# A hybrid block whose expert layer handles 56 instead of 48 tokens by gathered rows, with the choice of experts begun in the query projection

## The reference

```python
q = (xb @ w_q).reshape(T, PEER_HEADS, 2, PEER_HALF)            # 8 heads, 2 halves of 128
sc = jnp.einsum('thcd,hckd->thck', q, sub_keys)                # 128 keys for each half
s1, i1 = lax.top_k(sc[:, :, 0], PEER_TOPK)                     # the best 16 of each half
s2, i2 = lax.top_k(sc[:, :, 1], PEER_TOPK)
cand = (s1[..., :, None] + s2[..., None, :]).reshape(T, PEER_HEADS, PEER_TOPK * PEER_TOPK)
best, ci = lax.top_k(cand, PEER_TOPK)                          # the best 16 of 256 sums
...
u_sel = jnp.take(u_tab, idx, axis=0)                           # 128 rows of 16384 for each token
act = jax.nn.gelu(jnp.einsum('td,thkd->thk', xb, u_sel))
v_sel = jnp.take(v_tab, idx, axis=0)
return jnp.einsum('thk,thkd->td', g.astype(act.dtype) * act, v_sel)
```

## Time and profile before

| what | us |
|---|---|
| median of 3 runs | 1776.24 |
| lowest and highest | 1774.4, 1777.46 |
| the profiled execution: its own time | 1771.97 |
| its span, first to last instruction | 1769.7 |
| scoring's first product | 450.2 |
| value stage's first product | 1125.3 |

### The profile page before, as it was taken

How to read it: one execution, slowest core, us unless ns; L and a number is a source line. 1 busy time by engine, 2 the same in 40 slices (tenths; PEclk the granted TensorE clock), 3 DMA queues, 4 the chain that set the end, 5 groups by cost and what they waited for, 6 DMA issues and landing times. The chain is left out here.

```text
span 1769.7 us, 28855 instructions
## 1 busy us (share of the span) xinstructions
PE 1744.7 (99%) x10950; PEld 1655.2 (94%) x10950; DVE 1423.8 (80%) x2151; ACT 931.9 (53%) x1403; POOL 415.8 (23%) x293
## 2 busy tenths in 40 slices
PE   9999999999999999999999999999999999999997
PEld 7887778788999999999999999999999999999997
DVE  4556786575589899999999998688888888888995
ACT  5454574444456555555555545555555545555553
POOL 0002300020142133111111112023434433343341
PEclk9999999999999999999999999999999999999998
DMA  7765455678577677777777779899999999999992
GB/s 233 213 188 167 143 150 178 184 255 236 172 218 219 218 256 243 253 240 230 230 227 228 232 232 324 254 338 373 353 357 344 356 325 356 360 368 403 366 347 85
DMA packets 127138, 462.59 MB, mean 261 GB/s; under 512 B 14864, under 2 KB 14944, under 8 KB 126352
## 3 DMA queue, kind: packets, MB, share of 16 engines
q1 hardware_dynamic: 95760, 347.65, 60.5%
q0 software_dynamic: 30960, 112.64, 17.1%
q10 hardware_dynamic: 288, 0.55, 0.1%
HBM read 455.73 MB, written 5.05 MB: 260 GB/s over the span
## 5 line engine op out<-in xcount | busy, mean ns | idle before, releaser
L1641 PE MATMUL PS<-W,HI 128*128 128x416 f32 x2048 | 438.9, 354 | 1.4 <-DVE W L1222 0.8
L1601 PE MATMUL PS<-xT,HI 128*128 128x416 f32 x2048 | 438.4, 356 | 0.0
L682 ACT ACTIVATE HI<-V_RAW 128x1024 fp32r<-128x1024 f32 x256 | 271.7, 1062 | 282.6 <-PE PS L1641 151.4
L1641 PEld LDWEIGHTS PS<-W,HI 128*128 128x128 f32 x2048 | 366.1, 189 | 7.2 <-DVE OUTA L1256 1.9
L1601 PEld LDWEIGHTS PS<-xT,HI 128*128 128x128 f32 x2048 | 366.0, 189 | 2.9
L1146 DVE TENSOR_TENSOR V_LO<-V_RAW,HI 128x2048 fp32r<-128x2048 f32 x128 | 293.0, 2289 | 48.6 <-ACT HI L682 43.4
L682 ACT ACTIVATE HI<-RING_RAW 128x1024 fp32r<-128x1024 f32 x256 | 269.6, 1053 | 77.5 <-DMA RING_RAW<-u_t 72.0
L1153 DVE TENSOR_TENSOR RING_LO<-RING_RAW,HI 128x1024 fp32r<-128x1024 f32 x232 | 274.4, 1219 | 4.6 <-ACT HI L682 4.6
L819 DVE TENSOR_TENSOR LO<-RAW,HI 128x1024 fp32r<-128x1024 f32 x132 | 163.1, 1238 | 142.8 <-PE PS L1349 97.9
L1607 PEld LDWEIGHTS PS<-xT,RING_LO 128*128 128x128 f32 x2048 | 268.0, 191 | 3.7 <-DVE RING_LO L1153 2.2
L1646 PEld LDWEIGHTS PS<-W,V_LO 128*128 128x128 f32 x2048 | 269.4, 191 | 1.9 <-DVE V_LO L1146 0.8
(11 more groups left out here) (209 smaller groups left out, 1656.9 us busy)
## 6 DMA issues: line engine op xcount, KB each, us to landing
RING_RAW<-u_t SPq DMA_DIRECT2D x256, 512.0 KB
V_RAW<-peer_v SPq DMA_DIRECT2D x256, 512.0 KB
RAW<-w_in SPq DMA_DIRECT2D x80, 512.0 KB, 3.7
RAW<-w_out SPq DMA_DIRECT2D x32, 512.0 KB, 4.4
RAW<-wq_t SPq DMA_DIRECT2D x32, 512.0 KB, 4.8
x_spill<-X POOLq DMA_DIRECT2D x2, 1024.0 KB, 5.8
X1R<-x_spill POOLq DMA_DIRECT2D x8, 256.0 KB
X<-x SPq DMA_DIRECT2D x3, 512.0 KB, 8.4
```

The source lines that it names most:

```text
L682: nc.scalar.activation(HI[:, n % HI_SLOTS, :], raw_of(n), ACT.Copy).then_inc(top_ready, 1)
L1601: return mm(PS[:, j % S_BANKS, 0:2 * ND].rearrange("p (a t) -> p a t", a=2), HI[:, n % HI_SLOTS, kk * P:(kk + 1) * P], xT[:, k, :, 0:ND], ...
L1641: return mm(PS[:, V_BANKS[i], 0:2 * ND].rearrange("p (a t) -> p a t", a=2), HI[:, v % HI_SLOTS, i * P:(i + 1) * P], weights_of(v), start=v ...
```

## The change

NB_ goes from 16 to 24, so 56 tokens are gathered and ND is 200. The 24 tokens of B stand five times in 120 partitions, with 26 groups of picks instead of 16; half rows go from 192 to 232, of which 78 are in scoring. The order of the halves is now A's dots, A's sums, B's dots, B's sums (`half_of`), with two small activations (`A_GELU_AT` is step 111). The key scores are taken in the query projection, two columns of keys after every fourth unit (`pair_scores`), and the first 12 pieces of both tiles' choice run there on DVE; the other 58 pieces run in the steps 1 to 39. For the units 9, 11, ... 31 of the query projection POOL makes the low part instead of DVE. The loads of the keys move ahead for that. Spreading is the steps 43 to 92; `one_hots` is one comparison for both tables on DVE, and ACT multiplies the second by the gates in four operations (`gates_into`). It stands ahead of `apply_gates` now. The loops of the query projection are written out. Not shown: places in memory, semaphores, and the constants' other uses.

```diff
-NA, NB_ = 32, 16
+NA, NB_ = 32, 24
 NS = NA + NB_
 ND = T - NS
-GROUPS_A, GROUPS_B = P * NA // P, P * NB_ // P
+PICKS = PH * TOPK
+ROWS_A, ROWS_B = P // NA, P // NB_
+PB = ROWS_B * NB_
+GROUPS_A, GROUPS_B = PICKS // ROWS_A, -(-PICKS // ROWS_B)
 NG = GROUPS_A + GROUPS_B
-PICKS = PH * TOPK
...
-CHOICE0 = 2
-GATES_AT = (20, 48)
-PICKS_AT = (31, 58)
-ROWS_SAVED_AT, ROWS_BACK_AT = 32, 35
+EARLY = 12
+QUERY_BESIDE = range(WQ0 + 9, WQ_END, 2)
+CHOICE0 = 1
+
+
+def piece_steps():
+
+    steps, j = [], CHOICE0
+    rest = 2 * (PIECES - EARLY)
+    while len(steps) < rest:
+        steps += [j] * min(2 - j % 2, rest - len(steps))
+        j += 1
+    return [-1] * EARLY + steps[:PIECES - EARLY] + [-1] * EARLY + steps[PIECES - EARLY:]
+
+
+PIECE_STEPS = piece_steps()
+PIECE_COUNT = {j: PIECE_STEPS.count(j) for j in range(NKEYS)}
+PLAIN_STEP = {j: PIECE_COUNT[j] > 0 and all(k % PIECES in PLAIN for k in range(2 * PIECES) if PIECE_STEPS[k] == j)
+              for j in range(NKEYS)}
+BEST_PIECE = HC + 2 + PH
+GATES_AT = tuple(PIECE_STEPS[o * PIECES + BEST_PIECE] + 1 for o in range(TT))
+PICKS_AT = tuple(PIECE_STEPS[o * PIECES + PIECES - 1] + 2 for o in range(TT))
+ROWS_SAVED_AT, ROWS_BACK_AT = PICKS_AT[0] + 1, PICKS_AT[0] + 4
 TOKB = 4
 N_BATCH = ND // TOKB
-SPREAD0 = 60
+SPREAD0 = PICKS_AT[1] + 2
 SPREAD_END = SPREAD0 + N_BATCH
 FIRST_WEIGHTS_AT = SPREAD_END + 2
...
-HALF_STEPS = list(range(40, SPREAD0, 3)) + list(range(SPREAD0, SPREAD_END, 2)) + list(range(SPREAD_END, NKEYS - 7))
+HALF_STEPS = sorted([j for j in range(SPREAD0 - 3, SPREAD_END) if j % 3] + list(range(SPREAD_END, NKEYS - 7))
+                    + list(range(SPREAD_END, NKEYS - 7, 2)))
...
+A_DOTS, A_SUMS = 2 * GROUPS_A, 4 * GROUPS_A
+B_DOTS, B_SUMS = A_SUMS + 2 * GROUPS_B, A_SUMS + 4 * GROUPS_B
+A_GELU_AT = HALF_STEPS[A_DOTS - 1]
+B_GELU_AT = HALF_UNITS[B_DOTS - 1 - len(HALF_STEPS)]
+
+
+def half_of(k):
+
+    if k < A_SUMS:
+        return k < A_DOTS, k % A_DOTS // 2, k % 2
+    return k < B_DOTS, GROUPS_A + (k - A_SUMS) % (2 * GROUPS_B) // 2, k % 2
...
+            def keys(q):
+                pool.dma_start(KEYS[:, 4 * q:4 * q + 4, :], keys_t[:, 4 * q:4 * q + 4, :]).then_inc(keys_ready[q], 16)
+
+            pool.wait_ge(used, WQ0 + 1)
+            keys(0)
             pool.wait_ge(used, WQ0 + 2)
             for half in range(2):
                 cols = slice(half * HALF, (half + 1) * HALF)
                 pool.dma_start(FGAIN[:, cols], ffn_gain[:, cols].broadcast_to([P, HALF])).then_inc(fgain_ready, 16)
+            pool.wait_ge(used, WQ0 + 5)
+            keys(1)
...
-            for q in range(4):
-                pool.wait_ge(used, WQ0 + 14 + 2 * q)
-                pool.dma_start(KEYS[:, 4 * q:4 * q + 4, :], keys_t[:, 4 * q:4 * q + 4, :]).then_inc(keys_ready, 16)
-            pool.wait_ge(xg_saved, 16)
-            for r in range(P // NA):
-                pool.wait_ge(used, WQ0 + 22 + 2 * r)
-                pool.dma_start(X4[r * NA:(r + 1) * NA, :], xg_dram[0:NA, :]).then_inc(x4_ready, 16)
+            for n in QUERY_BESIDE:
+                pool.wait_ge(hi_ready, n + 1)
+                pool.wait_ge(used, n - (LO_SLOTS - 1))
+                nc.gpsimd.tensor_tensor(LO[:, n % 2, :], RAW[:, n % 4, :], HI[:, n % 4, :].bitcast(FP32),
+                                        ALU.subtract).then_inc(lo_ready[n % 2], 1)
+                if n == WQ0 + 9:
+                    keys(2)
+                if n == WQ0 + 17:
+                    keys(3)
+                if n - WQ0 in (21, 23, 25, 27):
+                    r = (n - WQ0 - 21) // 2
+                    pool.wait_ge(xg_saved, 16)
+                    pool.dma_start(X4[r * NA:(r + 1) * NA, :], xg_dram[0:NA, :]).then_inc(x4_ready, 16)
...
+            def pair_scores_out(q):
+
+                act.wait_ge(sc_done, q + 1)
+                nc.scalar.activation(SC[:, :, 2 * q:2 * q + 2, :],
+                                     PS[:, 4 + q % 4, :].rearrange("p (t a b) -> p t a b", t=TT, b=NKEYS), ACT.Copy)\
+                    .then_inc(sc_out, 1)
+
+            for m in range(4, N_WQ):
+                hi(WQ0 + m)
+                if m >= 9 and m % 4 == 1:
+                    pair_scores_out((m - 9) // 4)
...
+            def gates_into(b):
+
+                act.wait_ge(compared, b + 1)
+                for i in range(TOKB):
+                    t = b * TOKB + i
+                    ins = nc.scalar.activation(ONE[:, 1, i, :], ONE[:, 1, i, :], ACT.Copy, scale=EG[:, 2, t:t + 1])
+                ins.then_inc(ones, 1)
...
+            dve.wait_ge(xs_saved, 16)
+            for m in range(2, N_WQ + 2):
+                if m < N_WQ:
+                    lo(WQ0 + m)
+                c = (m - 3) // 2
+                if m % 2 and c >= 0:
+                    dve.wait_ge(used, WQ0 + 2 * c + 2)
+                    add_halves(QTQ[:, c, :], c % 2)
+                if m % 2 == 0 and 0 <= (m - 8) // 2 < EARLY:
+                    for o in range(TT):
+                        next(pieces[o])
+                        done[o] += 1
...
-                v.tensor_tensor(ONE1[:], IOTA[:].unsqueeze(1).broadcast_to([P, TOKB, NKEYS]),
-                                EG[:, 0, b * TOKB:(b + 1) * TOKB].unsqueeze(2).broadcast_to([P, TOKB, NKEYS]), ALU.is_equal)
-                for i in range(TOKB):
-                    t = b * TOKB + i
-                    ins = v.tensor_scalar(ONE2[:, 4 * i:4 * i + 4, :], IOTA[:].rearrange("p (q c) -> p q c", q=4),
-                                          EG[:, 1, t:t + 1], EG[:, 2, t:t + 1], ALU.is_equal, ALU.mult)
-                ins.then_inc(ones, 1)
+                t0 = b * TOKB
+                v.tensor_tensor(ONE[:], IOTA[:].unsqueeze(1).unsqueeze(1).broadcast_to([P, 2, TOKB, NKEYS]),
+                                EG[:, 0:2, t0:t0 + TOKB].unsqueeze(3).broadcast_to([P, 2, TOKB, NKEYS]), ALU.is_equal)\
+                    .then_inc(compared, 1)
...
-                if 0 <= b < N_BATCH:
-                    apply_gates(b)
                 if 0 <= b + 1 < N_BATCH:
                     assert done == [PIECES, PIECES]
                     one_hots(b + 1)
+                if 0 <= b < N_BATCH:
+                    apply_gates(b)
                 if b >= 0:
                     land(j)
-                if j in HALF_STEPS:
-                    half_rows(HALF_STEPS.index(j))
+                for k in range(len(HALF_STEPS)):
+                    if HALF_STEPS[k] == j:
+                        half_rows(k)
...
+            def pair_scores(q):
+
+                pe.wait_ge(tile_out, 2 * q + 2)
+                pe.wait_ge(keys_ready[q // 2], 16)
+                if q >= 4:
+                    pe.wait_ge(sc_out, q - 3)
+                for tt in range(TT):
+                    for c in (2 * q, 2 * q + 1):
+                        at0 = (2 * tt + c % 2) * NKEYS
+                        last = mm(PS[:, 4 + q % 4, at0:at0 + NKEYS], QTQ[:, c, tt * P:(tt + 1) * P], KEYS[:, c, :],
+                                  start=True, stop=True)
+                last.then_inc(sc_done, 1)
+
+            for m in range(N_WQ):
+                n = WQ0 + m
+                high_ready(n)
+                if m >= 4 and m % 2 == 0:
+                    pe.wait_ge(tile_out, m // 2 - 1)
+                column_unit(n, m // 2 % 2, low_ready(n),
+                            (lambda k: pe.wait_ge(tr_lo, 16 + max(2, k // 2 + 1))) if m < 2 else None)
+                if m >= 5 and m % 4 == 1:
+                    pair_scores((m - 5) // 4)
```

190 lines of the change are left out of this document (69 added, 121 removed).

## The result

The changed kernel takes **1810.88 us** (median; 1805.77 to 1811.19) and the kernel before 1775.32 beside it: ratio 1.0195, 95% interval 1.0171 to 1.022. Forecast were 1758.3 us and a range of 1747 to 1769. It is slower by 1.7 to 2.2%, and yet the profile says that its products did get cheaper.

What follows compares the result with a forecast made beforehand. The prediction took PE's own pace as the bound, busy for 1744.7 of 1769.7 us. Its terms summed to -17.9 us, which from the median of 1776.24 gave 1758.3 us, range 1747 to 1769.

Steps and rivals of the forecast that it cites:

- high products, both stages: Scoring and value stage: 4096 high products on PE move 16 columns fewer, 6.5 ns each, -26.6 us.
- low products: Scoring and value stage: low products go from 208 to 200 columns but stand on a floor, 0.
- choice on DVE: Scoring steps 24 to 28: DVE's sums of the choice run late and PE waits, +4 us.
- query: wait and clock: Query projection: PE stalls for POOL's first low part, +5.0 us, and the pause lowers its clock, +1.7.
- spreading's new loop: Spreading steps: the chain through DVE and ACT takes 5.5 us of a 5.6 us step and fits narrowly, 0.
- gathered halves, late: Scoring steps 93 to 119: three halves take 10.0 us against 9.44; between 0 and +4, taken as +2 us.
- value stage: Value stage: 154 halves instead of 150, loads and gathers at 364 GB/s where they were 352, costing 0.
- -1.8: Spreading: 50 batches instead of 52, 16 products fewer at 113 ns, -1.8 us.
- -2.2: Scoring: PE's old waits where the second tile's sums are chosen go away, -2.2 us.
- were it 0.15 longer: Spreading: with the loop 0.15 us longer, 50 steps would lose 7.5 us, less nearly 3 that PE's order leaves.
- more waits: Rival: the loop through ACT (+5), or gathers at the upper bound with a longer choice stall; 1763 to 1770, chance 0.22.
- the gathers become the bound: Rival: slow gathers in steps 93 to 119 make the kernel slower, +26 us in all, 1802; chance 0.05.

Runs made afterwards that it cites:

- Experiment 1: The changed kernel with VectorE's half row ahead of `land` and not behind it: ratio 1.0084 to the kernel before.
- experiment 6: Experiment 1 with ScalarE scaling the gates' table for two of four tokens and VectorE making the other two: ratio 1.002 to the kernel before.
- Experiments 3: The changed kernel with VectorE making both spreading tables and no scalings on ScalarE: ratio 1.0123 to the kernel before.
- 17: Experiments 3 with `apply_gates` ahead of `one_hots` again on VectorE: ratio 0.9987 to the kernel before.
- experiment 14: The changed kernel, unchanged, run again for its profile on another chip: 1806.4 us, ratio 1.0184 to the kernel before.
- 13: The kernel before, unchanged, run again for its profile on the chip of experiment 14: 1773.4 us.
- experiment 5: Experiment 1 with gathers of the second table's rows bringing 256 columns and not 1024: ratio 0.9969 to the kernel before.
- 10: Experiment 6 with GpSimd's query low parts from unit 13, and in the value stage five half-row slots for three, eight unit places for ten: ratio 0.9977.
- 15: 10 with four half-row slots in scoring, and three slots and ten unit places in the value stage: ratio 0.9924 to the kernel before.
- experiment 11: 10 with four slots for gathered half rows in the scoring in place of three: ratio 0.9929 to the kernel before.

## Why the prediction was wrong

The forecast's span was 1769.7 - 17.9 = 1751.8 us; the profiled one is 1809.4, 57.6 more. By its steps:

| step of the forecast | forecast | measured | miss |
|---|---|---|---|
| high products, both stages | -26.6 | -31.9 (steps 4.839 to 4.704, units 2.407 to 2.350) | -5 |
| low products | 0 | 0 (110 and 109 ns) | 0 |
| choice on DVE | +4 | +4.2 (steps 24 to 43: 4.914 for 4.704) | 0 |
| query: wait and clock | +6.7 | 3.1 to 3.5 of wait, and the clock as forecast (3 us at 0.50) | -2 |
| **spreading's new loop** | **0** (5.62 a step) | **6.44 a step, 50 steps** | **+41** |
| gathered halves, late | +2 | +15.2 (33 steps in 170.4 us) | +13 |
| value stage | 0 | time over PE's pace 18.2 us, before 8.7 | +9.5 |

These make 57. (The terms -1.8 and -2.2 are not in the table; nothing in the profile speaks against them.)

**The step that failed is "Spreading's new loop", priced at 0.** Two things were wrong in it. The size: four operations at 0.2 us each; they start 0.295 us apart. In the earlier trace rows two operations of ScalarE start 0.19 us apart, on 116 and 92 columns and without a scale, and I took that for the price of 128 columns with one. And the links: I followed ScalarE from `put_gates` straight to the copy, and left out that `land` on VectorE waits for `put_gates`, that the half row stands behind `land` in two steps of three, and the next sum behind that. The diff showed the cause: `apply_gates` had gone behind `one_hots`. I read it as nothing, since VectorE's work is the same in either order. But `apply_gates` releases `put_gates`, and the 1.6 us of tables were its cover. Experiment 1 shows the half row's place (29 us), and what it leaves is the size: 5.83 for 5.62, 10 us in 50 steps, which experiment 6 gets back (11 us) by halving ScalarE's share. So the two make up the 41. Experiments 3 and 17 together show the cover (24 us between them), 17 alone that both edits of the spreading undone give back 37 us. The break-even I had set was right ("were it 0.15 longer"): it was 0.82 longer, over five times that, and the price with it. Of the rivals none had this place; "more waits" had +5 for it.

**Gathered halves, late: the mechanism was right, the size was off.** I took three halves at 10.0 us against 9.44 and stopped at the upper bound of 4. From the sum of step 93 to that of step 120 two steps, with their three halves, took VectorE 10.56 us. The stretch ran at 341 GB/s, not at the 231 of the scoring before that I let speak for quicker gathers, and VectorE came into it some 3 us late from the spreading, so most of the 4 us that I counted as hidden were used up. It also had the clock once at 0.50 (about 3 us, from 1061), under 2 us of the 13. The fourth slot shows that it was the landing: the waits go, at 1.5 half rows a step.

**Value stage.** I had put "Loads and gathers come to 222 + 142 = 364 GB/s" beside a stretch of 60 us at 401, and said 0. The stage moved 350 in the mean where PE's own pace would ask for 361 (216 MB in 255 units of 2.350 us), and of the 14.5 us that the products gave there 5.0 arrived (4.5 in experiment 14 against 13). What failed here is that I took the rate of the best 60 us for that of the whole: with the engines nearly full (DMA share 0.96 to 1.02) stretches of 90 us moved from 352 to 390 GB/s, and the first one 323 at 0.93. Thin gathers with VectorE's work unchanged took 15 us off this stage (experiment 5, against 1), and two more slots, at the price of two places for units, 3 us at most (10, 15). The Trainium skill (DMA: Bandwidth & Descriptors, Bandwidth) puts one core's share of HBM at about 358 GB/s when both cores of a pair stream, and has 425 measured for a single core in a 16 MB transfer; this kernel runs on one core. The traces lie on both sides of 358: 339 to 351 over the whole stage in the kernels with whole gathers of 128 rows, 369 and 382 over 200 us in experiment 14 (from 1230 and from 1537 us), and 363 over 129 us of late scoring in experiment 11. So 358 is not shown as a limit here. The prediction's 141 us by that figure for the steps 93 to 119 was nearly met (140.1 us at 340 GB/s), but by luck: with a fourth slot the same steps took 129.0. The rival that the gathers become the bound was right in its direction for the value stage and the late scoring, 23 us of the 57, but its 1802 came from a gather of 11.5 us, where the median from issue to landing was 7.8 us for the first table's rows and 8.3 for the second's; the sign was turned by the spreading.

**The query.** PE's wait ended at 392.38, after 3.1 to 3.5 us and not 5.0:

```profile
384.26 4.77 POOL L458 TENSOR_TENSOR X<-X,FGAIN 56x1024 f32<-56x1024 f32 x2 [4.78 <-DMA X<-xs_spill]
389.33 0.55 POOL L460 DMA_DIRECT2D xg_spill<-X  x1 [0.29 <-POOL X L458]
389.89 2.43 POOL L464 TENSOR_TENSOR LO<-RAW,HI 128x1024 fp32r<-128x1024 f32 x1
```

The multiplication began when the earlier trace rows has it (384.26 for 384.49) and was done sooner, in 4.77 us for 5.78; and PE came to these low products at 389.1, later than the 388.5 of the sum. The clock behaved as forecast. Windows of the changed kernel (PEclk is third from the end):

```profile
389.00:392.50 3.50, 0.41 (x3) 0.13 (x1) 3.33 (x14) 0.10 (x1) 3.19 (x4) 0.96 0.48 122
392.50:395.50 3.00, 3.00 (x13) 2.90 (x14) 1.36 (x5) 0.00 (x0) 0.82 (x2) 0.50 0.69 198
395.50:398.50 3.00, 3.00 (x21) 2.70 (x20) 0.17 (x1) 1.54 (x2) 1.92 (x1) 0.98 0.65 254
```

After 3.1 to 3.5 us without a product, 3 us ran at 0.50, the lower of the two levels (1.2 GHz), with 13 products in them and then 21. That agrees with the Trainium skill (TensorE: Matmul & The Clock Gate, Why this matters for your kernels), by which a gap between bursts puts the engine back to half rate. After that the changed kernel's clock fell only once before the last 30 us, in the late scoring and not in the value stage.

**The chances.** 0.92 for faster rested on a sum whose largest unknown stood at 0 with 0.1 us to spare a step, times 50. A term like this belongs in the range with its whole price.

## What to carry over

When an edit changes the order of two operations on one engine, list what each of them releases on other engines, and what covered that work till now; an order with the same sum of work can cost half a microsecond in every step. Follow a loop through every in-order queue until it comes back to where it began, and count what stands behind each waiting instruction. Where a loop fits by 0.1 us and runs 50 times, take its operations' price from start to start from the same shape, and let the range carry the loop's price.
